# A two-layer hybrid decoder trunk: the state-space mixer without GpSimd and in another order, and experts with 1024-column blocks, an fp32r scatter and an end per token tile

## The chip, the cores and the metric

The kernel runs on one core of a Trainium2 chip. The metric is the device time of one execution in microseconds (us), lower is better. The core has five engines with instruction streams of their own: TensorE (PE, matrix products; PEld is its loading of the stationary operand), VectorE (DVE), ScalarE (ACT), GpSimd (POOL) and SyncE (SP), which issues the large transfers. Each engine runs its stream in order; semaphores join them. SBUF is the on-chip memory, and PSUM has eight banks of 128 partitions x 512 fp32 columns, in which TensorE leaves its results.

## The reference, cut to what matters

The input is x (1, 256, 1024), fp32. There are two layers and a final RMSNorm.

The even layer projects the normed input to u, q, k and v (512 columns each). u goes through a diagonal complex state-space model (32 groups of 16 channels with 64 states), v, q and k through causal attention of 8 heads; both are concatenated, projected and added, and a dense SwiGLU of width 2816 follows.

```python
abar_re = mag * jnp.cos(dt * ai); abar_im = mag * jnp.sin(dt * ai)
bu_re = jnp.einsum('gpc,bsgc->bsgp', bbar_re, ug)          # and bu_im
_, _, st_re, st_im = lax.associative_scan(combine, (a_re_t, a_im_t, bu_re, bu_im), axis=1)
y = (jnp.einsum('gcp,bsgp->bsgc', c_re, st_re) - jnp.einsum('gcp,bsgp->bsgc', c_im, st_im))
y = y.reshape(Bsz, S, S5_WIDTH) + d * uf
y = jax.nn.gelu(y); y = y * jax.nn.sigmoid(y @ glu_w + glu_b)
```

The odd layer has another pair of mixers (not touched here) and then a mixture of experts: a router picks 2 of 8 experts for each of 256 tokens; every expert is a SwiGLU of width 3584, and the outputs are added with the router's gates.

```python
logits = xt @ router; top_val, top_exp = lax.top_k(logits, TOP_K); gates = jax.nn.softmax(top_val)
yb = swiglu(x_pad[tok], w_gate[e], w_up[e], w_down[e])     # (silu(x @ w_gate) * (x @ w_up)) @ w_down
y = zeros.at[slot_tok].add(yb * slot_gate[:, None])
```

## The kernel before, in words

Activations are kept transposed (features on partitions, 256 tokens along the columns) in `hT` and `xnT`. Weights stream from HBM in 2 MB blocks into seven slots (`ring`, `ring2`); SyncE issues the load of a block when the block that had the slot before is used.

**Even mixer.** `plan` is one list of steps, written by hand, which TensorE, ScalarE and VectorE each walk in its order, taking the parts that are theirs. Ahead of it TensorE makes u (four tiles, L1581). VectorE works out the model's parameters on 16 partitions, waiting for ScalarE's sines (L615, L616, after the first copy of u); TensorE turns them (`turn_params`, L1600) and VectorE copies them at L1005. A chunk has LC = 4 steps, so a group has N4 = 64 chunks. VectorE then makes powers (`power`), B (L1037 to L1044) and the chunk's input operator `GT` (L1051 to L1056), while GpSimd makes the fractions of turns for the sine tables (L512 to L515), the decays (L517) and the output operands `HP` (L525 to L530). TensorE turns `GT` in 64x64 pieces (`turn_g`, L1639), makes chunk inputs (`chunk_u`, L1624) and chunk states (`chunk_states`, L1652). VectorE's `scans` rotate the states, scan them in two halves of 512 columns (L1066 to L1074) and rotate back; of this last part GpSimd does the first half (L535 to L540). `within_chunk` (L1669) builds a Toeplitz operator, `chunk_outputs` (L1686, L1689) applies it and the states, and `turn_outputs` (L1700) turns the result, which VectorE adds to u (L1092). Six projections (`proj`, L1581 and L1761) into banks 5 to 7, four ropes (L1770; VectorE L1126 to L1129) and ten attention steps (`attn`) are interleaved with these. An attention step u computes scores of unit u (L1717), the output of unit u-2 (L1727) and the transposes of unit u-1 (L1741); the softmax between them is VectorE's (L1103 to L1118) and ScalarE's (L636). The loads of the output weights (n = 5 and 6) wait for the states and for `M_done`.

**Experts.** Tokens of an expert are gathered into an item of at most 96 (`CAP`) slots; in this run there are eight items. An item takes 21 weight blocks: for each of seven chunks of 512 hidden columns a gate, an up and (one chunk later) a down block. `by_tokens` (L2172, L2174) multiplies the tokens, 32 at a time as the stationary operand, with 512 weight columns, spread over the four column quadrants of the array. After the gate product come silu (ScalarE, L904) and, after the up product, H (VectorE, L1513); `turn_hidden` (L2188) transposes H, three transposes a chunk, behind the next chunk's gate block. At the end of the last up block TensorE gathers the next item (L2154), transposes the item's gated one-hot matrix (L2232) and turns the last H. The item's output Y is scattered to tokens in two halves (`scatter`, L2161: fp32, two products of 512 columns each), one behind the next item's first gate block and one behind its first up block; VectorE adds each (`add_scattered`, L1485).

**End.** After the last item both tiles are scattered one after the other through the same banks 6 and 7, then squares of both tiles (L921), one root (L924), two scalings (L1535) and one store (L485).

Of the kernel before, what the change touches and what calls it, by code (L numbers as in the profile page):

```python
# [60 lines left out]
def constants():  # L61
# [15 lines left out]
    out["pick_out"] = (r == w % 32 // C5 * 64 + w // 32 * C5 + w % C5).astype(f)  # L77

# [65 lines left out]
def trunk(nc, a, consts_dram, out):  # L144
# [11 lines left out]
    def sem(name):  # L156
        if name not in sems:
# [4 lines left out]
                         "s5_w", "s5_states"],  # L162
             "s5_turned": ["s5_params_T", "c_T"],
             "s5_pool": ["s5_zero", "frac_ready", "d0_ready", "h_ready", "s5_states_pool"],
# [41 lines left out]
    def slot(s, w=KD * FB):  # L206
# [6 lines left out]
                               ("um", 4 * T), ("pT", 512), ("Hre", R5 * P), ("Him", R5 * P), ("G", R5 * P),  # L213
                               ("X", R5 * N4), ("M", R5 * N4), ("pow", 2 * R5 * 5), ("prm", 8 * R5)])
# [3 lines left out]
                                        ("Cn", 512), ("C", 512), ("Bz", 2 * (R5 * 32 + C5)), ("GT", R5 * N4)])  # L218
    assert end <= (SLOTS - PAIR_SLOTS) * KD * FB
    s5w, _ = carve(ring2, free_slots, [("ct", R5 * N4), ("st", R5 * N4), ("d0", R5 * N4), ("t", R5 * 5 * C5)])  # L220
    assert 3 * R5 * N4 + R5 * 5 * C5 <= NT * D + 16 * P + 2 * P
    att, _ = carve(xnT.rearrange("p k t -> p (k t)"), 0, [("rope", 1024), ("p", 1024)])
    stat = sb("stat", 64)
# [3 lines left out]
    Braw, CT = (pre[n].rearrange("p (m r c) -> p m r c", m=2, r=R5) for n in ("B", "C"))  # L227
    Craw = pre["Cn"].rearrange("p (m k x) -> p m k x", m=2, k=4)
    Bz = pre["Bz"].rearrange("p (m x) -> p m x", m=2)
    GT = [x.rearrange("p (r j c) -> p r j c", r=R5, j=LC) for x in (pre["GT"], L0["um"])]  # L230
    HP = [L0[n].rearrange("p (r x) -> p r x", r=R5) for n in ("Hre", "Him")]
    G_ = L0["G"].rearrange("p (r m x) -> p r m x", r=R5, m=2)
    XS = [L0["G"][:, R5 * N4 * m:R5 * N4 * m + R5 * N4].rearrange("p (r n) -> p r n", r=R5) for m in range(2)]
    X_, M_ = (L0[n].rearrange("p (r n) -> p r n", r=R5) for n in ("X", "M"))
    pw = L0["pow"].rearrange("p (m r k) -> p m r k", m=2, r=R5)
    prm = L0["prm"].rearrange("p (q r) -> p q r", q=8)
    wa, wb, w1, w2 = pre["GT"], L0["um"], ring2[:, free_slots + NT * D + 18 * P:][:, 0:R5 * N4], L0["M"]
# [71 lines left out]
    def flat(ap):  # L309
# [39 lines left out]
    MO, end = carve(arena, 0, [("xtok", NT * D), ("htok", NT * D), ("onehot", NT * CAP),  # L349
                               ("gated", NT * CAP), ("gatedT", T), ("silu", FM), ("H", FM),  # L350
# [139 lines left out]
    def _(pool):  # L490
# [9 lines left out]
        def cols(x):  # L500
            return x.rearrange("p (r n) -> p r n", r=R5)
# [1775 lines left out]
```

## Time and profile before

| | us |
|---|---|
| median of three runs | 1705.72 |
| lowest, highest | 1705.07, 1710.39 |
| the profiled execution | 1705.36 |
| its span, first to last instruction | 1703.5 |
| TensorE busy | 1580.5 (93%) |
| VectorE, ScalarE, GpSimd busy | 438.4, 283.5, 62.4 |
| mean granted TensorE clock | 0.956 |
| moved by transfers | 425.28 MB, mean 250 GB/s |

Busy time is the union of an engine's instructions. Matmuls overlap in the pipeline, so their durations add up to more than their busy time; what one costs is read from the distance of two starts. A clock of 1.00 is 2.4 GHz, 0.50 is 1.2 GHz. An fp32 product is recorded as two matmul instructions.

### The profile page before, as it was taken

What the parts mean: (1) busy time and instruction counts of PE and PEld (TensorE: products, weight loads), DVE (VectorE), ACT (ScalarE), POOL (GpSimd) and SP (SyncE); (2) the same over time, 40 slices, a digit from 0 to 9 for tenths busy, and PEclk for the clock granted to TensorE, in tenths of its full rate; (3) what the DMA queues carried; (4) which work ended last, traced back from release to release, by engine and by line L of the source; (5) the groups of instructions that cost most, each with busy time, mean ns of one, the idle gap of its engine ahead of it and who ended that gap; (6) DMA issues with size and microseconds to landing.
All of it is one profiled execution on the core that took longest, in us unless ns stands there. A gap on an engine that the chain in (4) does not pass through costs nothing.

```text
span 1703.5 us, 48100 instructions
## 1 busy us (share of the span) xinstructions
PE 1580.5 (93%) x22681; PEld 1469.7 (86%) x22681; DVE 438.4 (26%) x827; ACT 283.5 (17%) x467; POOL 62.4 (4%) x40
## 2 busy tenths in 40 slices
PE   7586999999974889899999999999999999999995
PEld 6555899998963778899999999999999999999994
DVE  4673244546648661200100100100100100001001
ACT  2113334434424111100000000000000000000001
POOL 0720000000000210000000000000000000000000
PEclk9798999999985999799999999999999999999997
DMA  9004345446310008299899999999999999999960
GB/s 305 1 1 150 127 173 196 174 149 223 119 50 1 3 2 309 104 379 382 327 384 380 327 375 367 350 376 360 350 380 361 352 379 359 351 379 347 361 249 26
DMA packets 184788, 425.28 MB, mean 250 GB/s; under 512 B 9770, under 2 KB 12948, under 8 KB 184468
## 3 DMA queue, kind: packets, MB, share of 16 engines
q1 hardware_dynamic: 182672, 420.59, 67.3%
q8 instruction: 180, 2.95, 0.7%
q10 hardware_dynamic: 1924, 1.64, 0.4%
q14 instruction: 12, 0.10, 0.0%
HBM read 421.17 MB, written 1.05 MB: 248 GB/s over the span
## 4 chain that ended last, share of the span: by engine, by line
PE 87%; DVE 9%; ACT 2%; issue 1%; DMA 0%; DVEq 0%; SPq 0%; ACTq 0%
PE bank L2174 33%; PE bank L2172 20%; PE bank L1819 5%; PE bank L1821 5%; PE bank L1820 5%; PE bank L1581 2%; PE bank L2154 2%; PE bank L2161 2%; PE bank L1794 2%; PE bank L2188 2%; PE bank L1807 1%; PE bank L1571 1%; PE bank L1812 1%; PE bank L1761 1%; DVE xnT L949 1%
## 5 line engine op out<-in xcount | busy, mean ns | idle before, releaser
L2174 PE MATMUL bank<-ring,yT 128*32 128x128 f32 x8064 | 893.6, 273 | 0.0
L2172 PE MATMUL bank<-ring,yT 128*32 128x384 f32 x8064 | 881.1, 487 | 1.0 <-ACT yT L877 1.0
L2174 PEld LDWEIGHTS bank<-ring,yT 128*32 128x32 f32 x8064 | 874.6, 110 | 0.0
L2172 PEld LDWEIGHTS bank<-ring,yT 128*32 128x32 f32 x8064 | 322.1, 109 | 21.2 <-issue 20.0
L1513 DVE TENSOR_TENSOR arena<-arena,bank 128x384 f32<-128x384 f32 x56 | 31.0, 553 | 717.6 <-PE bank L2174 717.6
L1821 PE MATMUL bank<-arena_r,ring_r 128*128 128x256 f32 x688 | 192.7, 280 | 0.0
L904 ACT ACTIVATE arena<-bank 128x384 f32<-128x384 f32 x56 | 27.5, 490 | 761.5 <-PE bank L2174 761.5
L1819 PE MATMUL bank<-yT_r,ring_r 128*128 128x256 f32 x512 | 144.1, 281 | 4.7 <-DVE arena_r L1164 4.7
L1820 PE MATMUL bank<-yT_r,ring_r 128*128 128x256 f32 x512 | 143.8, 281 | 0.0
L1821 PEld LDWEIGHTS bank<-arena_r,ring_r 128*128 128x128 f32 x688 | 130.3, 189 | 0.0
L1159 DVE TENSOR_TENSOR ring_r<-ring,ring_r 128x2048 fp32r<-128x2048 f32 (+1 forms) x46 | 98.9, 2153 | 112.7 <-ACT ring_r L697 112.5
L697 ACT ACTIVATE ring_r<-ring 128x2048 fp32r<-128x2048 f32 (+1 forms) x46 | 82.9, 1804 | 116.4 <-PE bank L1821 110.6
L1819 PEld LDWEIGHTS bank<-yT_r,ring_r 128*128 128x128 f32 x512 | 96.7, 189 | 5.5 <-issue 5.5
L1820 PEld LDWEIGHTS bank<-yT_r,ring_r 128*128 128x128 f32 x512 | 96.2, 188 | 0.0
L1819 PE MATMUL bank<-arena_r,ring_r 128*128 128x256 f32 x176 | 49.1, 279 | 0.0
L1820 PE MATMUL bank<-arena_r,ring_r 128*128 128x256 f32 x176 | 49.1, 279 | 0.0
L1581 PE MATMUL bank<-xnT,ring 128*128 128x256 f32 x192 | 44.2, 392 | 2.3 <-DVE xnT L949 2.3
L1581 PEld LDWEIGHTS bank<-xnT,ring 128*128 128x128 f32 x192 | 37.3, 196 | 8.3 <-DVE xnT L949 2.7
L1498 DVE COPY arena<-bank 32x128 f32<-32x128 f32 x48 | 14.1, 294 | 115.3 <-PE bank L2174 114.7
L1485 DVE TENSOR_TENSOR arena<-arena,bank 128x512 f32<-128x512 f32 x32 | 20.6, 684 | 87.6 <-PE bank L2161 87.6
L2161 PE MATMUL bank<-arena 96*128 96x512 f32 x64 | 34.3, 661 | 4.9 <-issue 3.5
L1562 PE MATMUL bank<-con 128*128 128x256 f32 x146 | 36.2, 403 | 0.9 <-ACT arena L872 0.8
(420 smaller groups left out, 1331.6 us busy)
## 6 DMA issues: line engine op xcount, KB each, us to landing
ring<-in_moe_w_gate SPq DMA_DIRECT2D x56, 2048.0 KB, 10.0
ring<-in_moe_w_up SPq DMA_DIRECT2D x56, 2048.0 KB, 10.4
ring<-in_moe_w_down SPq DMA_DIRECT2D x56, 2048.0 KB, 10.4
ring<-in_ffn_w_gate SPq DMA_DIRECT2D x5, 2048.0 KB, 7.9
ring<-in_ffn_w_up SPq DMA_DIRECT2D x5, 2048.0 KB, 7.8
ring<-in_ffn_w_down SPq DMA_DIRECT2D x5, 2048.0 KB, 7.6
ring<-in_o_w_in SPq DMA_DIRECT2D x5, 2048.0 KB, 7.8
ring<-in_e_w_in SPq DMA_DIRECT2D x4, 2048.0 KB, 16.8
```

Of the source, the lines that this page charges most:

```text
L697: act_.activation(pair(h, src.shape[1])[0], src, ACT.Copy).then_inc(sem("hi_done"), 1)
L1159: v.tensor_tensor(lo, src, hi.bitcast(f32), SUB).then_inc(sem("lo_done"), 1)
L1562: pe_.matmul(b[:, 0:2 * P], ident, con[:, 0:2 * P], start=True, stop=True)
L1581: last = pe_.matmul(dst(i)[0:width, :], w[:, k, i * P:i * P + width], xnT[:, k, :], start=(k == 0), stop=(k == KD - 1))
L1794: last = pe_.matmul(half(bank[2 + i // 2], i), view(n + i // 4)[:, k, (i % 4) * P:(i % 4) * P + P], yT[:, k, :], start=(k == 0), stop=(k = ...
L1819: pe_.matmul(dst, w[0], x[0], start=start, stop=False, skip_group_check=True)
L1820: pe_.matmul(dst, w[1], x[0], start=False, stop=False, skip_group_check=True)
L1821: return pe_.matmul(dst, w[0], x[1], start=False, stop=stop, skip_group_check=True)
L2154: last = pe_.matmul(bank[6 + k // 4][:, (k % 4) * CAP:(k % 4) * CAP + CAP], mtok[:, t, k * P:k * P + P], onehot[:, t, :], start=(t == 0), ...
L2161: last = pe_.matmul(bank[6 + i][:, :], MO["gatedT"][0:CAP, t * P:t * P + P], MO["Y"][0:CAP, FB * i:FB * i + FB], start=True, stop=True)
L2172: pe_.matmul(b[QUAD[m], 0:FM], x(m), w[:, 0:FM], start=start, stop=stop, skip_group_check=True)
L2174: last = pe_.matmul(b[QUAD[3], P * m:P * m + P], x(m), w[:, FM:FB], start=start and m == 0, stop=stop, skip_group_check=True)
```

## The change

In the even mixer GpSimd keeps one memset. Its other work goes to VectorE (fractions, `HP`, all of the last rotation) and ScalarE (decays, spreading B, zeros). ScalarE takes a sine of a constant right after the first norm, and the sines ahead of both copies of u. `turn_params` moves between the third and the fourth tile of u. `GT` skips power 0. `turn_g` transposes whole 128x128 pieces. The Toeplitz operator gives way to step kernels: `step_kernels` makes C A^j B for four steps, ScalarE spreads them to block-diagonal 128x128 operands `KB`, and `within_chunk` multiplies these with u itself, accumulating in banks 1 and 2, on which `turn_outputs` adds the turned outputs of `chunk_outputs`. `plan` is reordered, with the second half of V (`v`) and the new steps between the attention steps. The scratch of rope and softmax moves to weight slot 0.

In the experts a block is 512 rows x 1024 columns (the last of four chunks: 1024 rows x 512 columns), again 21 blocks an item. Silu, H and the transposes work on 768 columns at a time and so come four times an item. The scatter multiplies by a one-hot matrix (`mine`) in fp32r, with Y times the gate split into a high and a low part (`Yhi`, `Ylo`, VectorE); the gates reach the slots by two one-column products (`turn_mine`). The scatters stand behind the second gate block and the first up block. At the end the two tiles use different banks and are added, squared, scaled and stored one by one, and ScalarE takes one root of a constant ahead of it.

```diff
-    plan = [("proj", 0), ("params", 0), ("C", 0), ("X", 0), ("proj", 1), ("G", 0), ("proj", 2), ("S", 0)]
-    plan += [("proj", i) for i in (3, 4, 5)] + [("rope", i) for i in range(4)] + [("attn", 0), ("attn", 1), ("M", 0)]
-    plan += [("attn", 2), ("attn", 3), ("y", 0), ("attn", 4), ("attn", 5), ("out", 0)]
-    plan += [("attn", u) for u in range(6, KM * NT + 2)]
+    plan = [("C", 0), ("proj", 0), ("X", 0), ("G", 0), ("S", 0), ("proj", 1), ("rope", 0), ("rope", 1), ("proj", 2)]
+    plan += [("K", 0), ("proj", 3), ("rope", 2), ("rope", 3), ("proj", 4), ("attn", 0), ("v", 0), ("attn", 1), ("v", 1)]
+    plan += [("attn", 2), ("inner", 0), ("attn", 3), ("inner", 1), ("attn", 4), ("y", 0), ("attn", 5), ("y", 1)]
+    plan += [("attn", 6), ("out", 0), ("attn", 7), ("attn", 8), ("attn", 9)]
+    ROPE_BANK, PROJ_BANK = [7, 5, 5, 6], [5, 6, 6, 7, 7, 4]
...
@@ SyncE
             if n in (5, 6):
                 sp.wait_ge(*step("s5_states"))
-                sp.wait_ge(*step("s5_states_pool"))
-                sp.wait_ge(sem("M_done"), 2)
+                sp.wait_ge(*step("K_done"))
...
@@ ScalarE
+        act_.activation(stat[:, 0:1], C("eps"), ACT.Sin)
+        act.wait_ge(*step("s5_angle"))
+        act_.activation(small[6], small[5], ACT.Sin, scale=TWO_PI)
+        act_.activation(small[7], small[5], ACT.Sin, scale=TWO_PI / 2).then_inc(sem("s5_sin"), 1)
...
+            elif what == "K":
+                act.wait_ge(*step("K_done"))
+                for g in range(P // C5):
+                    last = act_.activation(KB[:, :, :, g, :].rearrange("p k j c -> p (k j) c"),
+                                           bank[4][:, 0:T].rearrange("p (x c) -> p x c", c=C5), ACT.Copy,
+                                           scale=C("group")[:, g:g + 1])
+                last.then_inc(step("kernel_ready")[0], 1)
...
@@ VectorE
+        link(v.tensor_tensor(cols(frac), C("time")[:, None, None, 0:N4].to_broadcast(shc),
+                             prm[:, 6, :].rearrange("p (a b) -> p b a", b=2)[:, :, :, None].to_broadcast(shc), MUL))
+        link(v.tensor_scalar(rn, frac, ROUND, ROUND, ADD, SUB))
+        v.tensor_tensor(frac, frac, rn, SUB).then_inc(step("frac_ready")[0], 1)
+        dve.wait_ge(*step("c_copied"))
...
+        times_powers([h.rearrange("p r (k c) -> p r k c", c=C5)[:, :, 1:, :] for h in HP],
+                     *(h[:, :, None, 0:C5].to_broadcast(shh) for h in HP), 1, ht_, 1, step("h_ready"))
...
@@ TensorE
+            for j in (2 * i, 2 * i + 1):
+                if j == 3:
+                    turn_params()
+                last = project(0, (j,), lambda j: half(bank[j // 2], j))
...
+        def within_chunk(h):
+            for k in (2 * h, 2 * h + 1):
+                for j in range(LC):
+                    o = T * (k % 2)
+                    pe_.matmul(bank[1 + h][:, o + N4 * j:o + T], KB[:, k, j].rearrange("p g c -> p (g c)"),
+                               uT[:, k, 0:LC - j, :].rearrange("p j n -> p (j n)"), start=(k % 2 == 0 and j == 0),
+                               stop=False, skip_group_check=True)
...
             elif what == "proj":
-                if i >= 3:
-                    pe.wait_ge(sem("proj_copied"), i - 2)
+                if i in (2, 4):
+                    pe.wait_ge(sem("proj_copied"), i)
+                if i == 3:
+                    pe.wait_ge(sem("rope_done"), 1)
...
@@ experts: blocks, scatter, turns
-    for c_ in range(NFC):
-        expert_blocks += [("moe_w_gate", c_), ("moe_w_up", c_)]
+    for c_ in range(NWC):
+        expert_blocks += blocks_of("gate", c_) + blocks_of("up", c_)
         if c_:
-            expert_blocks.append(("moe_w_down", c_ - 1))
+            expert_blocks += blocks_of("down", c_ - 1)
...
+            elif halves(c) == 2:
+                src = m[bass.ds(e, 1), x * FB:x * FB + FB, c * D:c * D + D]
...
+                v.tensor_scalar(hi, y, g, None, MUL).then_inc(sem("Yhi_ready"), 1)
+                dve.wait_ge(sem("Yhi_ready"), 2 * n + i)
+                v.scalar_tensor_tensor(lo, y, g, hi.bitcast(f32), MUL, SUB).then_inc(sem("Ylo_ready"), 1)
...
-                last = pe_.matmul(bank[6 + i][:, :], MO["gatedT"][0:CAP, t * P:t * P + P],
-                                  MO["Y"][0:CAP, FB * i:FB * i + FB], start=True, stop=True)
+                cols = slice(FB * i, FB * i + FB)
+                pe_.matmul(bank[b + i][:, :], mineT[0:CAP, t * P:t * P + P], Yhi[0:CAP, cols], start=True, stop=False)
+                last = pe_.matmul(bank[b + i][:, :], mineT[0:CAP, t * P:t * P + P], Ylo[0:CAP, cols], start=False,
+                                  stop=True)
...
+                if kind == "gate" and c == 0 and x == 1 and not peeled:
+                    pe.wait_ge(sem("Yhi_ready"), 2 * it + 1)
+                    pe.wait_ge(sem("Ylo_ready"), NT * it)
+                    scatter(0)
+                if kind == "up" and c == 0 and x == 0 and not peeled:
+                    pe.wait_ge(sem("scattered"), NT * it + 1)
+                    scatter(1)
+                if kind == "gate" and c and x == 0:
+                    turn_hidden(it, c - 1)
...
@@ end
+        act_.activation(MO["m12"][:, 14:15], C("eps"), ACT.Sqrt)
         for t in range(NT):
-            last = act_.activation(MO["xtok"][:, t * D:t * D + D], htok[:, t, :], ACT.Square,
-                                   accum_out=MO["m12"][:, 8 + t:9 + t])
+            act.wait_ge(sem("acc_final"), t + 1)
+            link(act_.activation(MO["xtok"][:, t * D:t * D + D], htok[:, t, :], ACT.Square,
+                                 accum_out=MO["m12"][:, 8 + t:9 + t]))
...
-            scatter(t)
+            scatter(t, 6 - 6 * t)
```

## Rows read from the trace of the kernel before

**Rows 1.** Busy time by stage: us, busy per engine (instructions), clock, share, GB/s.

```profile
20.80:122.30 101.50, 77.31 (x656) 59.95 (x656) 67.25 (x104) 16.05 (x23) 41.83 (x17) 0.88 0.21 76
122.30:171.30 49.00, 33.86 (x840) 25.27 (x841) 18.11 (x64) 15.43 (x53) 0.00 (x0) 0.81 0.37 131
...
705.50:1679.70 974.20, 974.16 (x16624) 933.27 (x16624) 67.48 (x159) 66.50 (x152) 0.00 (x0) 1.00 0.94 349
1679.70:1703.50 23.80, 6.52 (x8) 1.89 (x8) 6.98 (x13) 4.63 (x8) 0.00 (x0) 0.60 0.12 45
```

**Rows 2.** Timeline of TensorE, 20 to 75 us: start, duration, instruction, [idle before <-releaser].

```profile
20.77 22.67 PE L1581 MATMUL bank<-xnT,ring 128*128 128x256 f32 x96 [2.26 <-DVE xnT L949]
...
48.56 7.17 PE L1581 MATMUL bank<-xnT,ring 128*128 128x256 f32 x32
...
74.07 0.48 PE L1639 MATMUL bank<-con,ring 64*64 64x64 f32 x4 [18.34 <-DVE arena L1056]
```

**Rows 3.** Timeline of VectorE, 32 to 100 us.

```profile
32.65 0.28 DVE L991 SCALAR_TENSOR_TENSOR ring<-ring 16x128 f32<-16x128 f32 x1 [4.30 <-ACT ring L616]
...
43.95 0.26 DVE L1005 COPY arena<-bank 128x96 f32<-128x96 f32 x1 [7.88 <-PE bank L1600]
...
70.64 3.37 DVE L1056 TENSOR_TENSOR arena<-arena 128x1024 f32<-128x1024 f32 x1
...
93.07 0.68 DVE L1072 TENSOR_TENSOR arena<-arena 128x512 f32<-128x512 f32 x1
...
99.18 1.75 DVE L1072 TENSOR_TENSOR arena<-arena 128x512 f32<-128x512 f32 x1
```

**Rows 4.** Timeline of GpSimd, 73 to 98 us.

```profile
73.01 3.76 POOL L530 TENSOR_TENSOR arena<-arena,ring 128x1280 f32<-128x1280 f32 x1
96.21 1.27 POOL L535 TENSOR_TENSOR arena<-ring 128x512 f32<-128x512 f32 x1 [19.44 <-DVE arena L1074]
```

**Rows 5.** Chain of waits around the first scatter: start, duration, what.

```profile
829.08 1.91 PE bank L2161 x4
```

**Rows 6.** Timeline of TensorE around a later scatter and a turn of H.

```profile
1195.12 0.50 PE L2172 MATMUL bank<-ring,yT 128*32 128x384 f32 x3
...
1195.79 1.98 PE L2161 MATMUL bank<-arena 96*128 96x512 f32 x4
1197.71 0.52 PE L2172 MATMUL bank<-ring,yT 128*32 128x384 f32 x3
...
1209.54 0.50 PE L2172 MATMUL bank<-ring,yT 128*32 128x384 f32 x3
...
1209.86 0.50 PE L2172 MATMUL bank<-ring,yT 128*32 128x384 f32 x3
...
1210.85 0.52 PE L2172 MATMUL bank<-ring,yT 128*32 128x384 f32 x3
```

**Rows 7.** Timeline of TensorE in the dense SwiGLU: neighbouring fp32r products.

```profile
222.04 0.28 PE L1821 MATMUL bank<-arena_r,ring_r 128*128 128x256 f32 x1
222.16 0.28 PE L1819 MATMUL bank<-yT_r,ring_r 128*128 128x256 f32 x1
```

**Rows 8.** Busy time in a dense stretch of the experts, and the issues of down blocks.

```profile
1264.00:1300.00 36.00, 36.00 (x625) 35.07 (x617) 1.66 (x3) 1.78 (x4) 0.00 (x0) 1.00 1.04 391
...
ring<-in_moe_w_down SPq DMA_DIRECT2D x56, 2048.0 KB, 10.4
```

**Rows 9.** Timeline of the end, from the last down product (1679.7 us).

```profile
1683.21 2.74 PE L2161 MATMUL bank<-arena 96*128 96x512 f32 x4 [3.55 <-issue]
...
1687.32 3.78 PE L2161 MATMUL bank<-arena 96*128 96x512 f32 x4 [1.38 <-DVE arena L1485]
...
1694.72 1.28 ACT L924 ACT_TABLE_LOAD   x1
...
1699.05 0.40 SPq L485 DMA_DIRECT2D out_dram<-arena  x1
```

**Rows 10.** Busy time and granted clock after TensorE's wait for the norm.

```profile
20.00:24.00 4.00, 3.23 (x10) 2.73 (x11) 3.62 (x14) 0.00 (x0) 0.00 (x0) 0.74 0.98 384
```

More of the change, by code:

```diff
@@ L1054, in _, with times_powers @@
-        link(v.tensor_tensor(g2, b_im, a_re, MUL))
-        v.tensor_tensor(GT[0], GT[0], g1, SUB)
-        v.tensor_tensor(GT[1], GT[1], g2, ADD).then_inc(step("s5_gt")[0], 1)
+        shg = [P, R5, LC - 1, C5]
+        def times_powers(dst, x_re, x_im, first, tmp, sign, done):
+            a_re, a_im = (pw[:, m, :, first:first + dst[0].shape[2]][:, :, :, None].to_broadcast(list(dst[0].shape))
+                          for m in range(2))
+            v.tensor_tensor(dst[0], x_re, a_re, MUL)
+            v.tensor_tensor(tmp[0], x_im, a_im, MUL)
+            v.tensor_tensor(dst[1], x_re, a_im, MUL)
+            link(v.tensor_tensor(tmp[1], x_im, a_re, MUL))
+            v.tensor_tensor(dst[0], dst[0], tmp[0], (SUB, ADD)[sign])
+            v.tensor_tensor(dst[1], tmp[1], dst[1], (ADD, SUB)[sign]).then_inc(done[0], 1)
@@ L1586, in half @@
             return b[:, (i % 2) * T:(i % 2) * T + T]
-        norm(0)
-        pe.wait_ge(sem("xn_done"), 2)
-        loaded(0)
-        for i in range(2):
-            last = project(0, (2 * i, 2 * i + 1), lambda j: half(bank[j // 2], j))
-            last.then_inc(sem("u_done"), 1)
-        HALF = [slice(N5 * x, N5 * x + N5) for x in range(2)]
         def turn_params():
@@ L1702, in turn_outputs @@
+            for k in range(KM):
+                for j in range(LC):
+                    o = T * (k % 2) + N4 * j
+                    for q in range(4):
+                        last = pe_.matmul(bank[1 + k // 2][QUAD[q], o:o + N4], C("pick_out")[:, 32 * j:32 * j + 32],
+                                          Y5[:, 4 * k + q, :], start=False, stop=True, skip_group_check=True)
             last.then_inc(sem("y_turned"), 1)
-        S5_STEPS = {"params": turn_params, "C": turn_c, "X": chunk_u, "G": turn_g, "S": chunk_states,
-                    "M": within_chunk, "y": chunk_outputs, "out": turn_outputs}
@@ L2224, in run_item @@
-                if kind == "up" and c == NFC - 1:
+                        pe.wait_ge(sem("moe_silu"), NWC * it + c)
+                if kind == "up" and x == 0 and (c or not peeled):
+                    pe.wait_ge(sem("H_done"), NWC * it + c)
+                if kind == "down" and x == 0:
+                    pe.wait_ge(sem("ht_copied"), NWC * it + c + 1)
+                pe.wait_ge(loaded, count)
+                for k in range(nk):
+                    for i in range(n // FB):
+                        cols = w[:, k, FB * i:FB * i + FB]
+                        if kind == "down":
+                            last = by_tokens(bank[4 + i], lambda m: hidden(c, x, k, m), cols,
+                                             c == 0 and x == 0 and k == 0, c == LAST and k == nk - 1)
+                        else:
+                            kk = nk * x + k
+                            last = by_tokens(bank[i if kind == "gate" else 2 + i], lambda m: xg[:, kk, QUAD[m]], cols,
+                                             kk == 0, kk == KD - 1)
```

565 lines of the change are left out of this document (278 added, 287 removed).

## The prediction

> **What bounds the kernel now.** I read the busy time by stage first [rows 1]: four stretches, each with its own limit. From 705.5 to 1679.7 us (the experts) TensorE is busy for 974.16 of 974.20 us at full clock, so there only TensorE's own instructions cost time; transfers run beside it at 349 GB/s. From 20.8 to 122.3 us TensorE works for 77.3 us of 101.5, and from 122.3 to 171.3 us for 33.9 of 49.0: there the state-space chain and the attention chain decide. After 1679.7 us it works for 6.5 us of 23.8: a serial tail. The rest (171.3 to 705.5 us) is not touched by the diff. Then I read TensorE in time [rows 2]: 22.67 us for four tiles of u and two of projection 0, and then the largest hole of the program, 18.34 us until VectorE's L1056. So the start hangs on VectorE. Its rows [rows 3] say why it is late: 4.30 us for ScalarE's sine (behind a copy of u and a table load), 7.88 us for the turned parameters (queued behind projection 0), and then 128x1024 products of 3.37 us. The same line L1072 takes 0.68 us for 512 columns at 93.07 us, and 1.75 us at 99.18 us. What differs is GpSimd: it works beside all slow ones, to 76.8 us with products of up to 3.76 us, and again from 96.2 us [rows 4].
>
> The Trainium skill, "SBUF — State Buffer", section "Who interferes with whom", says that a VectorE instruction with two SBUF inputs and a GpSimd instruction that reads SBUF exclude each other. By that rule the 3.37 us are waits; were the price in the shape instead, rival A would follow. The pair of L1072 rows sides with the rule.
>
> **Part 1: the state-space mixer.** Without GpSimd I price VectorE by L1072: successive 512-column products there start 0.60 us apart, 0.533 of it for columns at 0.96 columns per ns. So 1024 columns are 1.13 us, 768 are 0.87, 256 are 0.34.
> The schedule that I work out, in us from the start:
> - ScalarE loads its sine table before the angle is there, and takes the sines ahead of u: VectorE's 4.30 us wait goes. Parameters ready at 31.8 instead of 36.1.
> - They are turned ahead of the last tile of u (free at 33.0): L1005 starts at 33.5, not 43.95. TensorE ends u at 37.1.
> - VectorE: powers 2.7 us, B 2.4, the 768-column products 6 x 0.87 + 0.1 = 5.3, so s5_gt at 44.0. Then it does GpSimd's work: fractions 2 x 1.13 + 0.6 + 0.2 = 3.1, and the output operands 6 x 1.13 + 0.1 = 7.0: h_ready at 54.1.
> - TensorE: C 1.1, projection 0 7.0 (7.17 in [rows 2], which overlaps its neighbours), chunk inputs 3.7: 48.9. Sixteen whole transposes with four copies between, 3.3: 52.2. States 3.9 (the same 128 instructions): 56.2. ScalarE's tables (3.2 us after the last copy) are ready at 55.4.
> - VectorE scans from 56.3: two halves of 6.1 and the states at full width, 7.0 (GpSimd had half of these before): 75.6. Beside it TensorE does projection 1, two ropes, projection 2 and the step kernels: 7.0 + 1.9 + 7.0 + 1.6, until 73.8.
> - A new wait: projection 3 uses rope 0's bank, and rope 0 is queued on VectorE behind the scans: 75.6 + 1.9 = 77.6. TensorE stands 3.8 us; everything is queued behind it. Projection 3 and the first half of V with two ropes: 84.6, 86.5, 93.5. The other ropes on VectorE end at 89.4, under that.
> - Attention starts at 93.5, not 122.3. Seven steps cost TensorE about 2.0 to 2.2 us each, with the 0.5 us for o_copied inside; unit 0 has half. Into their latencies go V's second half 2 x 3.45, inner 2 x 2.15 (1280 columns at four cycles), outputs 2 x 2.0, and the turn 3.3 (128 small instructions; before, 32 wide ones took 1.9). A softmax takes 3 to 4.2 us from its scores; each interval with a filler is 4.1 to 4.8, so nothing of it shows. Steps 0 to 6 with all fillers: 30.6 us, until 124.1. Then VectorE adds the outputs (4 x 0.34) before it may scale unit 6, as in the kernel before; two steps without fillers end at 132.4 to 133.
> Against 171.3 that is 38.5 us. Some 50 hand-overs of 0.03 to 0.1 us that I did not list, and a possible clock dip, take 1.5: 37 us. Bounds: 25 us (all attention steps as in the bare stretch of before, 3.7 us and more) and 42 us. The loads of the output weights now wait for 75.6 us instead of 138.7, far ahead of their use. ScalarE's new work (d0 1.0, spreading B 1.3, eight kernel copies 2.4) falls into its idle time, before 41.6 and at 73.8 to 76.2; without that cover the 2.4 us would stand before V's second half.
>
> **Part 2: the experts.** The period of an item: scatters start at 829.08 and, three items later, at 1195.79 [rows 5, 6]: 122.24 us. The products themselves stay: each pair of half-steps of 384 columns starts 2 x 0.323 apart (1209.54, 1209.86 in [rows 6]), which is four cycles per column at 2.4 GHz; 168 of 0.6457 are 108.5. The rest is interruptions.
> - Scatter: products start 0.323 apart, so the one after 1195.12 was due at 1195.45, and comes at 1197.71 [rows 6]: 2.26 us lost; the second of that item loses 2.11. Columns at four cycles are 1.71 of it, 0.48 is drain and fill. In fp32r two neighbours of 256 columns start 0.12 apart at one cycle per column [rows 7]; four products of 512 are 4 x 0.22 = 0.9, with 0.47 again 1.35. Gain 0.83, twice an item, in seven items: 11.6 us. No row shows an fp32r product between fp32 ones. Bounds: gain 1.3 each (18 us) if no drain is left, and a loss of 1.7 each (-24 us) if each of the four costs what fp32 costs. I take the row nearest to it, an fp32r product.
> - Hidden turns: the next product was due at 1210.18 and comes at 1210.85: 0.67 us for three transposes. Before six such, besides the one in the gather sequence; now three with six transposes, 0.67 + 3 x 0.14 = 1.09. Gain 0.75 an item, 6.0 us in eight. Between 0 and 8 us.
> - The gate column of the item: two one-column products more, four instructions of 0.11: loss 0.45 an item, 3.6 us. Between 0 and 6.
> - Yhi and Ylo are VectorE's: some 3.4 us after the item's last block, while TensorE does two gate blocks, 10.3 us, before the scatter asks. One block less of cover would still hide them. The gate and up steps wait for H of the chunk before, now with 10 us of blocks between.
> Sum: 14 us; the stage goes from 974.2 to 960. Transfers: 352 MB in 960 us is 367 GB/s; a stretch of 36 us shows 391 [rows 8], and seven slots of depth cover the rest. They stay hidden.
>
> **Part 3: the end.** Before, from the last product: 3.5 us to the scatter, 2.74, adding 1.28, then the second 3.78 at half clock, 1.28, two squares 2.2, the table 1.28, root 0.3, two scalings 2.5 and the store 4.45 [rows 9]. After: 4.2 (the split comes in), each scatter 4 x 0.44 at half clock, both without a wait between; adding, squaring and root of tile 0 (1.3, 1.2, 0.3) while tile 1 comes; tile 1's add ends at 9.0, square and root 10.5, scaling 12.0, a half store 3.3: 15.3. Gain 8.5 us, between 6 and 11.
>
> The Trainium skill, "ScalarE: Activation LUTs", section "What ACT_TABLE_LOAD costs", gives 2.66 us for a switch with its drain; the row of the load is 1.28 here. By the page the end would gain 1.4 us more.
>
> **The sum.** 37 + 14 + 8.5 = 59.5. Span 1703.5 - 59.5 = 1644.0. The profiled run took 1705.36, so 1.86 lie around the span: 1645.9; the median of before is 0.36 above that run: 1646.
>
> **Rivals.**
> A. The 3.3 us of VectorE belong to the broadcast shapes, not to GpSimd. For: every such product of before is slow. Against: L1072 and the L1080 to L1085 group, slow only while GpSimd runs. The 768-column products would take 6 x 2.5 (+9.6), two of the fractions +4, the operands 6 x 3.3 (+13): h_ready at 80, scans 24 later: 1670.
> B. The loads become the bound of the experts. For: the engines of the transfers are already busy for a share of 0.94 of the stage [rows 1]. Against: 391 GB/s in the dense stretch [rows 8]. Were today's mean rate all that the queue gives, part 2 is lost: 1660.
> The Trainium skill, "HBM Reference", section "Specifications (TRN2)", gives about 358 GB/s effective per core, and more for a core alone. By 358 the stage would take 984 us: 1670. The row of 391 speaks for the core alone.
> C. TensorE falls to half clock. After its wait at 18.5 to 20.8 us the granted clock was 0.74 on the mean of 20 to 24 us, part of it thus at 1.2 GHz [rows 10], and four tiles cost about 1.9 us more. The new 3.8 us wait could do that to projection 3 (+3: 1649); with attention too sparse as well, its 28 us of work double: 1674.
> The Trainium skill, "TensorE: Matmul & The Clock Gate", part 1, says that the array's clock is halved after idleness. It speaks for the +3, and for nothing of the rest while fillers keep it working.
> D. Slower than before: the gate and up blocks are now 512 rows of 4 KB, 14,336 bytes apart. If these come worse than today's 1024 rows of 2 KB, the experts wait. The other gains are 45.5, so this decides from a stage of 974.2 + 45.5 = 1020 us, which is 345 GB/s; at 335 GB/s the stage takes 1051 us, and the kernel 1737. Against: down blocks already have 4 KB rows and land as fast, in 10.4 us [rows 8].
> E. The change does not do what it says: fp32r between fp32 runs at fp32's cost, -24 instead of +11.6: 1682.
>
> **How the numbers follow.** Forecast 0.67, with its own range 1636 to 1657; A 0.12, C 0.08, B 0.06, E 0.04, D 0.03. The range 1632 to 1669 holds the forecast, most of C and B and the edge of A. 0.3% (5.1 us) is what a measurement can tell. Only D gives slower: faster 0.95, same 0.01, slower 0.04.
>
> **What would show it.** VectorE products of 1024 columns near 1.2 us and L1005's copy near 33.5 us; a TensorE wait of about 4 us for rope 0; the output projection starting near 133 us; scatters 119 to 120.5 us apart; fp32r scatter products starting 0.22 us apart; no TensorE wait for a load; 15 to 16 us from the last down product to the end. Wrong if VectorE's products stay near 3 us, if landing times pass 20 us, or if the projection starts after 145 us.

## The result, and the profile after

The changed kernel takes 1645.85 us (median of 4 runs, 1645.62 to 1646.46) against 1705.4 us: ratio 0.9645, 95% interval 0.9627 to 0.9663. The forecast was 1646. Its profiled execution took 1645.62 us with a span of 1643.8 us.

By stage, the columns as in [rows 1] (start; attention; the code between, of which the diff touches only the last step, the first gather, which goes to other banks; experts; end):

```profile
20.90:94.80 73.90, 66.82 (x590) 52.40 (x591) 56.75 (x113) 17.82 (x33) 0.00 (x0) 0.95 0.44 160
94.80:134.17 39.37, 31.31 (x409) 21.37 (x409) 18.35 (x60) 17.06 (x55) 0.00 (x0) 0.94 0.16 55
134.17:671.12 536.95, 479.55 (x4506) 442.01 (x4506) 269.42 (x459) 174.49 (x225) 18.10 (x16) 0.92 0.34 121
671.12:1629.87 958.75, 958.75 (x16656) 937.65 (x16656) 76.44 (x181) 70.57 (x180) 0.00 (x0) 1.00 0.93 354
1629.87:1643.80 13.93, 2.85 (x9) 1.79 (x8) 8.64 (x15) 6.05 (x13) 0.00 (x0) 0.67 0.20 78
```

| stretch | before | after | gain | forecast |
|---|---|---|---|---|
| start to output projection | 171.32 | 134.17 | 37.15 | 37 |
| middle | 534.15 | 536.95 | -2.8 | 0 |
| experts | 974.2 | 958.75 | 15.4 | 14 |
| last product to the end | 23.85 | 13.93 | 9.9 | 8.5 |
| span | 1703.5 | 1643.8 | 59.7 | 59.5 |

**The start.** Timeline of VectorE, 32 to 56 us, the answer to [rows 3]: the turned parameters, the last product of `GT`, the last of `HP`, and the first step of the scan.

```profile
32.55 0.26 DVE L1022 COPY arena<-bank 128x96 f32<-128x96 f32 x1 [0.63 <-PE bank L1640]
...
41.82 0.95 DVE L1073 TENSOR_TENSOR arena<-arena 128x768 f32<-128x768 f32 x1
...
51.61 1.22 DVE L1073 TENSOR_TENSOR arena<-arena 128x1024 f32<-128x1024 f32 x1
55.01 0.69 DVE L1106 TENSOR_TENSOR ring<-bank,ring 128x512 f32<-128x512 f32 x1 [2.18 <-ACT ring L625]
```

The copy comes 11.4 us earlier, its wait for TensorE is 0.63 instead of 7.88 us, and a product of 1024 columns takes 1.22 us, where 3.37 stood. The only wait left here is for ScalarE's tables.

Timeline of TensorE from the states to the output projection, the answer to [rows 2]:

```profile
51.76 2.09 PE L1702 MATMUL bank<-arena 64*64 64x64 f32 x128 [0.69 <-ACT arena L664]
...
69.67 1.10 PE L1715 MATMUL bank<-arena,ring 128*32 128x64 f32 x64
76.46 9.66 PE L1629 MATMUL bank<-xnT,ring 128*128 128x256 f32 x32 [5.69 <-DVE arena L1164]
...
121.91 1.99 PE L1748 MATMUL bank<-arena,con 128*32 128x64 f32 x128
...
126.69 0.44 PE L1788 MATMUL bank<-con,ring 128*128 128x128 f32 x2 [1.56 <-DVE ring L1140]
...
129.67 0.70 PE L1774 MATMUL bank<-arena 128*64 128x128 f32 x4 [2.54 <-ACT arena L644]
...
134.17 7.04 PE L1873 MATMUL bank<-yT,ring 128*128 128x256 f32 x27 [0.43 <-issue]
```

The 18.34 us hole is gone. In its place stands a wait of 5.69 us for rope 0 (L1164), and behind it projection 3, the same 32 products as projection 0's 7.17 us in [rows 2], takes 9.66. Behind the turn of the outputs (L1748) two waits of the softmax show.

**The experts.** Chain of waits through one item (start, duration, what), the answer to [rows 5] and [rows 6]:

```profile
1039.69 0.43 PE bank L2228
...
1090.32 0.80 PE bank L2261 x6
...
1122.70 0.80 PE bank L2261 x6
...
1128.88 3.74 PE bank L2220 x32
...
1133.48 0.25 PE bank L2240
...
1159.82 0.43 PE bank L2228
1160.25 0.23 PE bank L2229
...
1160.94 0.25 PE bank L2240
```

A scatter half is 0.43 + 3 x 0.23 = 1.12 us instead of 1.91, and from scatter to scatter an item takes 1159.82 - 1039.69 = 120.13 us instead of 122.24. Transfers keep up. Busy time in 360 us of the stage, and the issues of the blocks (median us to landing at the end), which answer to [rows 8] (the issues of up blocks have the median of the gate blocks, 9.4):

```profile
800.00:1160.00 360.00, 360.00 (x6249) 351.79 (x6248) 30.86 (x72) 26.23 (x70) 0.00 (x0) 1.00 0.97 369
```

```profile
ring<-in_moe_w_gate SPq DMA_DIRECT2D x56, 2048.0 KB, 9.4
ring<-in_moe_w_down SPq DMA_DIRECT2D x56, 2048.0 KB, 9.8
```

**The end.** Timelines of TensorE, VectorE, ScalarE and SyncE, the answer to [rows 9]:

```profile
1633.54 0.47 PE L2228 MATMUL bank<-arena_r 96*128 96x512 f32 x1 [3.67 <-DVE arena_r L1543]
1633.84 0.39 PE L2229 MATMUL bank<-arena_r 96*128 96x512 f32 x1
...
1635.75 0.63 PE L2229 MATMUL bank<-arena_r 96*128 96x512 f32 x1
```

```profile
1634.74 1.28 DVE L1521 TENSOR_TENSOR arena<-arena,bank 128x512 f32<-128x512 f32 x2 [1.34 <-PE bank L2229]
1636.42 1.29 DVE L1521 TENSOR_TENSOR arena<-arena,bank 128x512 f32<-128x512 f32 x2 [0.40 <-PE bank L2229]
...
1639.45 1.28 DVE L1583 SCALAR_TENSOR_TENSOR arena<-arena 128x1024 f32<-128x1024 f32 x1
```

```profile
1631.64 1.28 ACT L936 ACT_TABLE_LOAD   x1
```

```profile
1639.14 1.97 SPq L503 DMA_DIRECT2D out_dram<-arena  x2
```

The second tile is added 1.68 us behind the first; before, its products started 1.37 us after the end of the first scatter and took 3.78. The table load now lies beside VectorE's split of Y, ahead of the scatter, and the first tile is stored while VectorE scales the second.

### The profile page after: what moved, and what is told of

It reads as the page before. It is cut to its first block, busy times and chain, and to the rows that moved or that the text cites. A ratio compares the mean times of both kernels' runs of the same rounds, so it can differ in the third digit from the quotient of the medians.

```text
span 1643.8 us, 47174 instructions
## 1 busy us (share of the span) xinstructions
PE 1550.2 (94%) x22217; PEld 1464.2 (89%) x22217; DVE 439.0 (27%) x857; ACT 294.0 (18%) x515; POOL 19.3 (1%) x21
## 3 DMA queue, kind: packets, MB, share of 16 engines
q8 instruction: 176, 2.88, 0.7%
## 4 chain that ended last, share of the span: by engine, by line
PE 87%; DVE 9%; ACT 2%; issue 1%; DMA 0%; ACTq 0%; SPq 0%; DVEq 0%
PE bank L2242 34%; PE bank L2240 20%; PE bank L1885 5%; PE bank L1887 5%; PE bank L1886 5%; PE bank L2220 2%; PE bank L1860 2%; PE bank L2261 1%; PE bank L1629 1%; PE bank L1873 1%; PE bank L1795 1%; PE bank L1878 1%; PE bank L2228 1%; PE bank L1619 1%; DVE xnT L966 1%
## 5 line engine op out<-in xcount | busy, mean ns | idle before, releaser
L2242 PEld LDWEIGHTS bank<-ring,yT 128*32 128x32 f32 x8064 | 876.5, 110 | 0.0
L2240 PEld LDWEIGHTS bank<-ring,yT 128*32 128x32 f32 x8064 | 299.8, 109 | 11.7 <-issue 10.5
L902 ACT ACTIVATE yT<-bank 128x384 f32<-128x384 f32 x56 | 25.0, 491 | 560.5 <-PE bank L2261 560.5
L1533 DVE COPY arena<-bank 32x128 f32<-32x128 f32 x24 | 7.1, 294 | 159.4 <-PE bank L2242 159.2
L2220 PEld LDWEIGHTS bank<-arena 128*128 128x128 f32 x288 | 34.9, 202 | 2.7 <-issue 1.6
```

The costliest lines, as they stand in the source:

```text
L902: last = act_.activation(flat(ht[:, i if c < LAST else 2]), bank[6 + i][:, 0:FM], ACT.Copy)
L2220: last = pe_.matmul(bank[1 + 2 * (k // 4)][:, (k % 4) * CAP:(k % 4) * CAP + CAP], mtok[:, t, k * P:k * P + P], onehot[:, t, :], start=(t = ...
L2240: pe_.matmul(b[QUAD[m], 0:FM], x(m), w[:, 0:FM], start=start, stop=stop, skip_group_check=True)
L2242: last = pe_.matmul(b[QUAD[3], P * m:P * m + P], x(m), w[:, FM:FB], start=start and m == 0, stop=stop, skip_group_check=True)
```

## Experiments

Each time is compared with runs of the kernel before on the same chip: 1704.24 us for the first four kernels, 1704.02 for the next four, 1703.68 for the last four. The brackets behind a time give its ratio to that and the 95% interval. Diffs are against the changed kernel. It was itself timed again only with the last four, and took 1647.56 there; so against its 1645.85 a difference of 2 us in the first eight is no evidence, and I go by positions in the traces there.

### Each half alone: s5_only and experts_only

s5_only has the experts and the end of the kernel before, experts_only its mixer:

```diff
-    for c_ in range(NWC):
-        expert_blocks += blocks_of("gate", c_) + blocks_of("up", c_)
+    for c_ in range(NFC):
+        expert_blocks += [("moe_w_gate", c_), ("moe_w_up", c_)]
```

```diff
-    plan = [("C", 0), ("proj", 0), ("X", 0), ("G", 0), ("S", 0), ("proj", 1), ("rope", 0), ("rope", 1), ("proj", 2)]
...
+    plan = [("proj", 0), ("params", 0), ("C", 0), ("X", 0), ("proj", 1), ("G", 0), ("proj", 2), ("S", 0)]
```

> The kernel before with the state-space part of the change alone, experts and end as before. Theory (the parts add): the output projection starts 37 us earlier, the rest is as before, so 1705.7 - 37 = 1669 (1666 to 1672; the clock of the unchanged middle can move it by 2 to 3). Rival (the parts hide each other, the start gains more and the experts lose): 1660 or less, or 1675 and more.

> The kernel before with the experts' part and the end of the change alone. Theory: experts 15 us and end 10 us less: 1681 (1678 to 1684). Rival: the end gains because the last transfers or the clock stand better after the new start; then the tail here is over 17 us and the time 1687 or more.

Measured: 1668.76 us (0.9787, 0.9764 to 0.981) and 1681.33 us (0.9861, 0.9837 to 0.9884). The gains are 35.5 and 22.9 us, together 58.4 against 59.6 for both at once: within the scatter the halves add up, and neither pays for the other. The traced execution of experts_only was the slowest of its four (1686.41 us); its end took 15.9 us, under the 17 of the rival, and 1.58 of that is a pause inside the scatter whose cause the trace does not show.

### GpSimd at work beside VectorE: gpsimd_beside

```diff
+        pool.wait_ge(*step("s5_b"))
+        hflat, beside = hT.rearrange("p k t -> p (k t)"), yT_flat[:, 0:1280]
+        for _ in range(8):
+            link(pl.tensor_tensor(beside, hflat[:, 0:1280], hflat[:, 768:2048], MUL))
+        pool.sem_inc(sem("beside_done"), 1)
...
+            if what == "attn" and i == 0:
+                act.wait_ge(sem("beside_done"), 1)
```

Eight products are added whose result is not used; VectorE's own instructions stay as they are.

> The changed kernel with eight products of 1280 columns on GpSimd, SBUF to SBUF into memory that is free until the attention, started with s5_gt's products on VectorE. Theory (VectorE's slow products of before were waits for GpSimd): VectorE's products that lie beside them take 3 us and more, not 0.95 and 1.22, GpSimd works about 27 us, the output operands are late by some 14 to 17 us, and the time is 1660 (1655 to 1664). Rival A (the price was in the broadcast shapes, and fell because the new shapes are others): VectorE's rows stay at 0.95 and 1.22 and the time at 1646.

Measured: 1663.6 us (0.9756, 0.9735 to 0.9778). Timelines of GpSimd and of VectorE:

```profile
38.88 28.64 POOL L522 TENSOR_TENSOR yT<-hT 128x1280 f32<-128x1280 f32 x8 [37.21 <-DVE arena L1067]
```

```profile
38.83 0.96 DVE L1075 TENSOR_TENSOR ring<-ring,arena 128x768 f32<-128x768 f32 x1
39.71 3.65 DVE L1076 TENSOR_TENSOR arena<-arena 128x768 f32<-128x768 f32 x1
...
61.49 3.28 DVE L1096 TENSOR_SCALAR ring<-ring 128x1024 f32<-128x1024 f32 x1
64.81 3.80 DVE L1097 TENSOR_TENSOR ring<-ring 128x1024 f32<-128x1024 f32 x1
68.53 1.21 DVE L1075 TENSOR_TENSOR arena<-arena 128x1024 f32<-128x1024 f32 x1
```

Nothing but GpSimd's work differs from the changed kernel (ScalarE's new wait comes over 45 us after that work has ended), and the product of 768 columns goes from 0.95 to 3.65 us. The cost does not follow VectorE's columns: 768 take 3.65 us and 1024 take 3.80, about one GpSimd product (28.64 / 8 = 3.58), and eight slow VectorE instructions stand beside eight of GpSimd. It looks as if each waits for one of the other's; the trace gives GpSimd's eight in one row only, so the single pairs are not shown. The price is in the neighbour and not in the shape: rival A is refuted. No run takes GpSimd away from the kernel before itself, but the changed kernel's products for `HP` have the form of L1051 to L1056 (1024 columns, a broadcast power as a factor) and take 1.22 us. Eight instructions that took 7.6 us take 28.8, and the output projection starts at 153.70 instead of 134.17 (u took 12.31 us in this execution, not 10.63, which is 1.7 of it at most).

The neighbour alone is not enough either. In the kernel before, GpSimd and VectorE at 97 us:

```profile
97.45 1.27 POOL L536 TENSOR_TENSOR ring<-arena,ring 128x512 f32<-128x512 f32 x1
97.82 0.68 DVE L1069 TENSOR_TENSOR arena<-bank,ring 128x512 f32<-128x512 f32 x1
```

This product lies wholly beside one of GpSimd and costs its 0.68 us, as it did at 91.75 us without GpSimd: one of its inputs is in PSUM. L1072 at 99.18 [rows 3] has both in SBUF and takes 1.75.

The Trainium skill, "SBUF — State Buffer", section "Who interferes with whom", says this of products with two SBUF inputs, and also that a `tensor_scalar` in a two-port mode shuts GpSimd out and is shut out. By that page L1096, with one input, is slow too if it runs in such a mode; the trace agrees, 3.28 us instead of 0.69.

### Parameters late again: late_params

```diff
+            if i == 0:
+                act.wait_ge(*step("s5_angle"))
+                act_.activation(small[6], small[5], ACT.Sin, scale=TWO_PI)
...
-                if j == 3:
-                    turn_params()
...
+                if i == 0:
+                    turn_params()
```

The sines go behind the first copy of u, the turn of the parameters behind projection 0.

> The changed kernel with two of its moves undone: the sines come behind the first copy of u with their table load, and the parameters are turned behind projection 0, as in the kernel before. VectorE then copies them at about 45 us, 12.3 later. Slack of the input operator 6 us and of the output operands 2.2 us. Theory (this chain sets the start of the scans): scans at 65 instead of 55, all that follows 10 us later: 1656. Rival (TensorE's projections set the pace and VectorE has room): under 3 us.

Measured: 1654.31 us (0.9709, 0.9685 to 0.9733), and the scans start at 65.52 us. Timeline of VectorE:

```profile
32.59 0.28 DVE L1008 SCALAR_TENSOR_TENSOR ring<-ring 16x128 f32<-16x128 f32 x1 [4.29 <-ACT ring L594]
...
45.17 0.26 DVE L1022 COPY arena<-bank 128x96 f32<-128x96 f32 x1 [9.16 <-PE bank L1640]
```

The waits of [rows 3] are back with the order. Of 12.6 us at the copy, 9.5 arrive at the output projection (143.68): the two edits of order are worth about a quarter of the 37 us, GpSimd's absence and the rest of the reordering the remainder, which no run splits further.

### The new wait before projection 3: warm_wait and free_bank

warm_wait fills the wait with twelve products that nobody reads; free_bank takes away what makes it, the shared bank.

```diff
+                    pe.wait_ge(sem("S_read"), 2)
+                    keep_warm(bank[0], 12)
                     pe.wait_ge(sem("rope_done"), 1)
```

```diff
-    ROPE_BANK, PROJ_BANK = [7, 5, 5, 6], [5, 6, 6, 7, 7, 4]
+    ROPE_BANK, PROJ_BANK = [7, 5, 5, 6], [5, 6, 6, 0, 7, 4]
...
-                    pe.wait_ge(sem("rope_done"), 1)
+                    pe.wait_ge(sem("S_read"), 2)
```

> The changed kernel with twelve products of 256 columns that nobody reads, on a free bank, in TensorE's wait before projection 3. Theory (of the 2.5 us that projection 3 takes longer than projection 2, all is half clock after the wait): its row is 7.1 to 7.2 us instead of 9.66, and the time is 1643.5. Rival (the fill costs as much as it brings, since it ends after rope 0): 1646.

> The changed kernel with projection 3 in bank 0, which is free after the scans have read the states, instead of bank 7, which waits for VectorE's rope 0. Theory (the wait and its half clock are on the path): no 5.7 us wait, projection 3 at full clock, attention starts at 87.5 to 88 instead of 94.8 us, 1639 (1637.5 to 1640.5). Rival (VectorE's ropes, queued behind the scans until 78.3 us, are next and take most of it): under 3 us gained, 1643 and more.

Measured: 1643.6 us (0.9642, 0.9621 to 0.9663) and 1638.0 us (0.9606, 0.9585 to 0.9627). Timeline of TensorE in warm_wait, then in free_bank:

```profile
71.01 5.45 PE L1610 MATMUL bank<-con 128*128 128x256 f32 x24
76.75 7.17 PE L1629 MATMUL bank<-xnT,ring 128*128 128x256 f32 x32 [0.30 <-DVE arena L1164]
```

```profile
70.72 7.17 PE L1629 MATMUL bank<-xnT,ring 128*128 128x256 f32 x32
78.48 1.95 PE L1834 MATMUL bank<-arena,con 128*128 128x512 f32 x4 [0.59 <-DVE arena L1164]
```

With TensorE busy until 76.5 us projection 3 takes 7.17 us again, not 9.66: the 2.5 us are clock and nothing else. Its mean granted clock was 0.74 in the changed kernel (76.5 to 86.1 us) and is 1.00 here. Without the wait the attention starts at 87.23 instead of 94.80, so the wait and the clock behind it cost 7.6 us.

The price of such a wait is not one number. In the seven traces with a wait of 5.68 or 5.69 us the 32 products took 9.24 to 10.12 us. Behind longer waits they took less: 8.68 behind 8.02 us in late_params, 8.61 behind 14.25 in gpsimd_beside.

The Trainium skill, "TensorE: Matmul & The Clock Gate", part 1, has the rule that idleness halves the clock; these two traces agree (0.74 behind the wait, 1.00 without it).

### The turn of the outputs one step later: out_later

```diff
-    plan += [("attn", 6), ("out", 0), ("attn", 7), ("attn", 8), ("attn", 9)]
+    plan += [("attn", 6), ("attn", 7), ("out", 0), ("attn", 8), ("attn", 9)]
```

> The changed kernel with the turn of the outputs behind attention step 7 instead of ahead of it, so that VectorE scales unit 6 before it adds the outputs. Theory (the 1.56 and 2.54 us waits of the tail come from VectorE's 2.1 us of adding in front of the scaling): tail 2 to 2.5 us shorter, 1643.5. Rival (the adding then stands before the scaling of unit 7 and costs the same): 1646.

Measured: 1645.33 us, from 1641.21 to 1647.37 (0.9644, 0.9618 to 0.967): no verdict by time, and a miss. The trace tells why. From the first attention step (96.09) to the output projection (134.18) it takes 38.1 us instead of 39.4, a gain of 1.3 where 2 to 2.5 were expected; and this execution came to the attention 1.3 us late. Busy time and granted clock, 20 to 24 us, of out_later and then of the changed kernel:

```profile
20.00:24.00 4.00, 2.69 (x6) 2.19 (x7) 3.69 (x14) 0.00 (x0) 0.00 (x0) 0.65 0.98 385
```

```profile
20.00:24.00 4.00, 3.11 (x14) 2.77 (x15) 3.62 (x15) 0.00 (x0) 0.00 (x0) 1.00 1.00 386
```

The first 48 products of u took 12.23 us instead of 10.63. The edit does not reach them; the clock does: the changed kernel itself took 10.63 us for them in its first trace and 12.31 in its second. A gain of 1.3 us is smaller than this scatter. Why it is only 1.3 shows in TensorE's timeline:

```profile
130.82 1.11 PE L1788 MATMUL bank<-con,ring 128*128 128x128 f32 x4 [2.54 <-DVE ring L1140]
```

The rival was half right: the adding (2.11 us at 127.99) now stands before the scaling of unit 7, and TensorE waits 2.54 us for that.

### One fp32 product, or one fp32r product: scatter_fp32 and scatter_high

Both leave out the low part of Y. scatter_fp32 also keeps the high part and the one-hot matrix in fp32, so its products are those of the kernel before; scatter_high keeps them in fp32r.

```diff
-                v.scalar_tensor_tensor(lo, y, g, hi.bitcast(f32), MUL, SUB).then_inc(sem("Ylo_ready"), 1)
+                dve.sem_inc(sem("Ylo_ready"), 1)
...
-                pe_.matmul(bank[b + i][:, :], mineT[0:CAP, t * P:t * P + P], Yhi[0:CAP, cols], start=True, stop=False)
-                last = pe_.matmul(bank[b + i][:, :], mineT[0:CAP, t * P:t * P + P], Ylo[0:CAP, cols], start=False,
+                last = pe_.matmul(bank[b + i][:, :], mineT[0:CAP, t * P:t * P + P], Yhi[0:CAP, cols], start=True,
```

> The changed kernel with the scatter back in fp32: one product of unrounded Y times gate for each half instead of two in fp32r; VectorE skips the low part. Theory (fp32r saves 0.55 and 0.85 us at the two scatters of an item): 14 scatters x 0.70 = 10 us, and 1 to 2 at the end: 1657. Rival (the gain of an item comes from the new places of the scatters and the longer blocks, not from fp32r): within 3 us of 1646.

> Leaves out the low part of Y in the scatter (Ylo is neither made nor multiplied), so two fp32r products a half instead of four. If what an fp32r product costs between fp32 ones is its 0.23 us, an item saves 4 x 0.23 = 0.92, seven items 6.4, and the end 1.3 of VectorE and about 1 of TensorE: 1637. Rival: the price is in going over from fp32 to fp32r and back, and the number of products matters little: 1643.

Measured: 1659.94 us (0.9738, 0.9714 to 0.9762), and 1639.13 us (0.962, 0.9607 to 0.9633), 8.4 us under the changed kernel beside it. Chain of waits of scatter_fp32, then of scatter_high:

```profile
1043.50 1.91 PE bank L2228 x4
...
1165.21 1.91 PE bank L2228 x4
```

```profile
1038.17 0.66 PE bank L2228 x2
...
1157.37 0.66 PE bank L2228 x2
```

A half costs 1.91, 1.12 and 0.66 us with fp32, four and two fp32r products; the periods are 121.71, 120.13 and 119.20 us, apart by just twice that. So a further fp32r product is 0.23 us, and going over from fp32 costs 0.2 once, not per product. scatter_fp32 came out 3 us above its forecast: a half lost 0.79 us and not 0.70, and its end is 2.5 us longer from the first scatter product on, where the eight records of fp32 take 5.37 us. scatter_high's gain is the price of the low part of Y, which it leaves out.

### The last scatter through one pair of banks: end_one_bank

```diff
+            if t:
+                pe.wait_ge(sem("acc_final"), t)
-            scatter(t, 6 - 6 * t)
+            scatter(t, 6)
```

> The last scatter of tile 1 goes through the banks of tile 0 again and waits until tile 0 is added. The products of tile 1 start at 1634.54 in the changed kernel and would start behind the add, near 1636.1, so tile 1's add comes 1.6 us later and all behind it too: 1647.5. Rival: what the end gained came from the root, the table and the store by tile alone, and the second pair of banks gives nothing: 1645.9. If the wait costs the clock as well: 1649.

Measured: 1648.09 us (1647.25 to 1649.38) beside the changed kernel's 1647.56 (1646.72 to 1648.09): higher by 0.5 us, with overlapping runs, so the time alone leaves it unclear. Timeline of VectorE in end_one_bank:

```profile
1634.53 1.28 DVE L1521 TENSOR_TENSOR arena<-arena,bank 128x512 f32<-128x512 f32 x2 [1.37 <-PE bank L2229]
1637.98 1.29 DVE L1521 TENSOR_TENSOR arena<-arena,bank 128x512 f32<-128x512 f32 x2 [2.17 <-PE bank L2229]
```

The second add follows the first by 3.45 us instead of 1.69, and the end is 1.8 us longer by the trace, as expected. The earlier part of that execution was shorter by more (its first gather started 2.0 us before that of the changed kernel beside it, 663.99 against 666.03).

### The best version: best_both, with after_again beside it

Both edits of free_bank and out_later; after_again is the changed kernel itself.

```diff
-    ROPE_BANK, PROJ_BANK = [7, 5, 5, 6], [5, 6, 6, 7, 7, 4]
+    ROPE_BANK, PROJ_BANK = [7, 5, 5, 6], [5, 6, 6, 0, 7, 4]
...
-    plan += [("attn", 6), ("out", 0), ("attn", 7), ("attn", 8), ("attn", 9)]
+    plan += [("attn", 6), ("attn", 7), ("out", 0), ("attn", 8), ("attn", 9)]
```

> The changed kernel itself, as the measure for the small differences beside it: 1645.9, within 1 us.

> Both edits to the state-space mixer's order: projection 3 in bank 0 and the turn of the outputs behind attention step 7. The first alone gave 1638.0. The second shortened the stretch from the first attention step to the output projection by 1.3 us (38.1 instead of 39.4) although its time did not move beyond its scatter. If the two are independent: 1636.7. Rival: the turn's place is worth nothing in the time and what it seemed to give was the clock: 1638.

Measured: after_again 1647.56 us (0.967, 0.9656 to 0.9683), 0.7 us outside what I allowed; best_both 1637.35 us (0.9608, 0.9595 to 0.9621), 10.2 us under it. The expected 9.2 and the measured 10.2 are one within the scatter. The attention takes 38.10 us here (87.62 to 125.72) and 39.38 in free_bank: the turn's 1.3 us are there in the trace. In the time they are not shown: the ratio is 0.9608, and free_bank's was 0.9606, so the times leave the rival open, and the gain that they do show is free_bank's.

## Why the prediction was right

**The start (37 forecast, 37.15 measured).** The rows of VectorE came as priced: the copy at 32.55 (33.5), products of 1.22 and 0.95 us, starts 1.13 and 0.87 apart, `GT` done at 42.8 (44.0), `HP` at 52.8 (54.1). The choice on which the sum hung was to price VectorE by the one row of [rows 3] without GpSimd beside it; gpsimd_beside shows that this was the cause. Single terms were off and cancelled:
- The states took 2.1 us, not 3.9, and the step kernels 1.1, not 1.6. TensorE was thus ready for projection 3 at 70.8, not 73.8, and only waited longer: 5.69, not 3.8 us. Rope 0 came at 76.4 (77.6).
- The small part of rival C happened, 2.5 us (3 forecast), more than the 1.5 us that I had kept for clock and hand-overs together.
- Attention started at 94.80 (93.5) and took 39.4 us (39). The turn was 1.99 us, not 3.3; adding the outputs on VectorE was 2.13 us, not 1.36, and that lengthened what follows. Up to attention step 7 (123.83) it took 29.0 us (30.6), and the tail behind it 10.3 (8.7): two errors that cancel.

**The middle (0 forecast, -2.8 measured).** I took unchanged code to cost what it cost. Its 4506 matmul instructions are the same but for the banks of the last 32, the first gather. The clock of these was 0.88 before and 0.62 after. Timeline of TensorE at the first gather, of the kernel before and then of the changed one:

```profile
700.14 4.31 PE L2154 MATMUL bank<-arena 128*128 128x96 f32 x32 [0.26 <-DVE arena L1490]
```

```profile
664.18 5.92 PE L2220 MATMUL bank<-arena 128*128 128x96 f32 x32 [0.38 <-DVE arena L1526]
```

These 1.6 us are part of the 2.8. Up to the gather the stretch took 528.8 us before and 530.0 after, and the fourteen traces spread over 528.5 to 531.0. The changed mixer does not make the gather slow: five traces have this row at 4.0 to 4.4 us and nine at 5.9 to 6.0, with kernels with and without it in both groups. For the experts' part this is open: both traces with the old experts (before, s5_only) are among the five, and of the twelve with the changed ones only three.

**The experts (14 forecast, 15.4 measured).** All three terms can be read from the chain in an item (forecast per item in brackets):
- Scatter: 2 x (1.91 - 1.12) = 1.58 us (forecast 1.66), confirmed by scatter_fp32. Rival E is refuted: with fp32r products at fp32's cost the kernel would be slower than scatter_fp32.
- Turns: in the kernel before two chunks with a turn each take 32.67 us (its turns start at 1120.86, 1137.19 and 1153.53), the double chunk with one turn 1122.70 - 1090.32 = 32.38. Three of these gain 0.87 (0.75).
- The gate column: the gather sequence took 1175.72 to 1180.01 = 4.29 us before and takes 1128.88 to 1133.48 = 4.60: loss 0.31 (0.45).
Together 2.14 us an item; measured 122.24 - 120.13 = 2.11. Over seven scatters and eight items the terms are 11.1, 7.0 and -2.5 us, where I had 11.6, 6.0 and -3.6. B and D are refuted by landings of 9.4 to 9.8 us (10.0 to 10.4 before), and by 369 GB/s without a wait of TensorE. My 367 GB/s for the stage put all 352 MB of the blocks into it; the first are loaded ahead of it, and the stage moved 354 GB/s.

**The end (8.5 forecast, 9.9 measured).** Two terms were mis-sized. I priced all eight scatter products at half clock, 0.44 us; the first four came 0.24 us apart, at full clock, and from the first product to tile 1's add it is 2.88 us, not 3.52. And the split of Y was done sooner: the scatter started 3.67 us after the last product, not 4.2. Together 1.2 of the 1.4 us; the last store, 3.1 us and not 3.3, is the rest. The table load cost its 1.28 us and no more: in the kernel before the load lay from 1694.72 to 1696.00, and the root started at 1696.02.

So the sum of 59.5 met 59.7 with errors of +0.15, -2.8, +1.4 and +1.4. The mechanisms held, apart from the middle, for which I had put nothing. That the total hit within a microsecond is luck: the error of the middle cancels those of the experts and the end.

## What to carry to other kernels

When an instruction of VectorE has two durations in one trace, look at what GpSimd does beside each, and whether both read SBUF, before pricing it by shape; in gpsimd_beside each product on GpSimd made one on VectorE 2.6 to 2.7 us longer, and would itself have cost VectorE some 1.4 us (an estimate from the 1.13 us between two starts of 1024 columns). When a reorder frees an engine early, look for the bank or buffer that the next step shares with something queued late: here one bank index cost 7.6 us. Price an interruption in a dense stream of products by its columns plus one fixed changeover, and check unchanged stretches for the clock before giving them zero.

## What the runs showed of the hardware

- VectorE's instructions whose inputs all lie in SBUF become about as long as those of GpSimd beside them, which read SBUF too: 0.95 us becomes 3.65, 0.69 becomes 3.28. A product with one input in PSUM kept its 0.68 us beside GpSimd.
- Four fp32r products of 512 columns between fp32 products cost 1.12 us, two 0.66, the same columns as two fp32 products 1.91.
- A wait of 5.69 us left the next 32 products 2.5 us longer (2.1 to 3.0 in seven traces), at a mean clock of 0.74; with TensorE kept busy in it they took 7.17 us. Waits of 8.02 and 14.25 us cost the products behind them only 1.5.
- The granted clock of the same instructions differs from one execution to the next: 10.63 or 12.31 us for 48 products of u in two traces of the changed kernel, and 4.0 to 4.1 or 5.9 to 6.0 us for the gather in traces with the same experts. Executions of one kernel differ here by 1 to 8 us, and such rows are among what differs in those that were traced.
